# A hybrid decoder trunk: scores between tiles replaced by a recurrent state carried from tile to tile

## The reference

```python
S_t = diag(a_t) S_{t-1} + k_t v_t^T ; o_t = S_t^T q_t
    b = jnp.cumsum(ai, axis=2)
    diff = b[:, :, :, None, :] - b[:, :, None, :, :]
    decay = jnp.exp(jnp.where(causal, diff, -jnp.inf))
    scores = jnp.einsum('bhtc,bhsc,bhtsc->bhts', qi, ki, decay)
    o_intra = jnp.einsum('bhts,bhsv->bhtv', scores, vi)
    o_inter = jnp.einsum('bhtc,bhcv->bhtv', qi * jnp.exp(b), state)
```

## Time and profile before

| | |
|---|---|
| median of 3 runs | 2428.96 us (2427.64 to 2429.24) |
| the profiled execution, its own time | 2428.29 us |
| its span in the profile | 2426.6 us |
| granted TensorE clock, mean | 0.998 |
| TensorE busy | 2393.7 us, 99% |
| VectorE busy | 1939.1 us, 80% |
| ScalarE busy | 1202.9 us, 50% |

### The profile page before, as it was taken

How to read it: one execution, slowest core, us unless ns; L and a number is a source line. 1 busy time by engine, 2 the same in 40 slices (tenths; PEclk the granted TensorE clock), 3 DMA queues, 4 the chain that set the end, 5 groups by cost and what they waited for, 6 DMA issues and landing times.

```text
span 2426.6 us, 34798 instructions
## 1 busy us (share of the span) xinstructions
PE 2393.7 (99%) x13375; PEld 2082.1 (86%) x13375; DVE 1939.1 (80%) x2589; ACT 1202.9 (50%) x1787; POOL 50.7 (2%) x79
## 2 busy tenths in 40 slices
PE   8999999999999999999999999999999999999997
PEld 6888888888777888999999999988888888888885
DVE  6777777788887447988888888899999999995456
ACT  6445444444445235666666666643333333345345
POOL 4000000000000000000000000000000000000111
PEclk9999999999999999999999999999999999999999
DMA  6323323333324234666666666697564575633322
GB/s 176 87 73 82 86 70 85 87 84 81 79 74 152 92 131 137 182 204 200 199 197 196 197 196 196 205 353 253 198 232 160 191 257 195 229 131 116 112 85 99
DMA packets 381406, 373.71 MB, mean 154 GB/s; under 512 B 5532, under 2 KB 311352, under 8 KB 379224
## 3 DMA queue, kind: packets, MB, share of 16 engines
q1 hardware_dynamic: 381240, 371.88, 48.0%
q10 hardware_dynamic: 32, 0.01, 0.0%
HBM read 304.76 MB, written 67.11 MB: 153 GB/s over the span
## 4 chain that ended last, share of the span: by engine, by line
PE 62%; DVE 4%; ACT 1%; issue 1%; DMA 1%; DVEq 0%; ACTq 0%; SPq 0%
PE bank L2323 20%; PE bank L2325 20%; PE bank L2324 20%; DVE w_lo L2064 1%; DMA ring<-in_w_down 0%; DVE h L2110 0%; DVE w_lo L1927 0%; ACT w_hi L1143 0%; DVE w_lo L2201 0%; PE bank L2708 0%; PE bank L2603 0%; DVE gate_e L2227 0%; DVE h L2230 0%; PE bank L2401 0%; ACT gate_inv L1355 0%
## 5 line engine op out<-in xcount | busy, mean ns | idle before, releaser
L2323 PE MATMUL bank<-u_hi,w_hi 128*128 128x512 f32 x896 | 361.8, 404 | 3.4 <-DVE w_lo L1466 2.0
L2323 PE MATMUL bank<-w_hi,forms 128*128 128x512 f32 x896 | 349.4, 390 | 1.1 <-DVE h L2110 1.1
L2325 PE MATMUL bank<-u_hi,w_lo 128*128 128x512 f32 x896 | 349.8, 390 | 0.0
L2324 PE MATMUL bank<-u_lo,w_hi 128*128 128x512 f32 x896 | 349.2, 390 | 0.0
L2325 PE MATMUL bank<-w_hi,forms 128*128 128x512 f32 x896 | 348.7, 389 | 0.0
L2324 PE MATMUL bank<-w_lo,forms 128*128 128x512 f32 x896 | 348.6, 389 | 0.0
L2323 PE MATMUL bank<-xs,w_hi 128*128 128x256 f32 x1024 | 289.9, 283 | 1.4 <-DVE w_lo L1927 0.9
L2324 PE MATMUL bank<-xs,w_hi 128*128 128x256 f32 x1024 | 289.6, 283 | 0.0
L2325 PE MATMUL bank<-xs,w_lo 128*128 128x256 f32 x1024 | 289.5, 283 | 0.0
L1273 ACT ACTIVATE w_hi<-ring 128x1024 fp32r<-128x1024 f32 x124 | 132.0, 1066 | 214.6 <-PE bank L2325 140.4
L1466 DVE TENSOR_TENSOR w_lo<-w_raw,w_hi 128x2048 fp32r<-128x2048 f32 x70 | 160.0, 2286 | 63.2 <-ACT w_hi L874 63.0
(11 more groups left out here) (315 smaller groups left out, 5235.1 us busy)
## 6 DMA issues: line engine op xcount, KB each, us to landing
w_raw<-in_w_in SPq DMA_DIRECT2D x56, 1024.0 KB, 5.6
forms_scratch<-stage SPq DMA_DIRECT2D x32, 1792.0 KB, 11.4
forms<-forms_scratch SPq DMA_DIRECT2D x56, 1024.0 KB, 8.3
ring<-in_w_down SPq DMA_DIRECT2D x39, 1024.0 KB, 5.3
w_raw<-in_w_up SPq DMA_DIRECT2D x32, 1024.0 KB, 7.8
raw<-in_w_up SPq DMA_DIRECT2D x32, 1024.0 KB, 8.0
w_raw<-in_w_down SPq DMA_DIRECT2D x25, 1024.0 KB, 5.1
ring<-in_w_pg SPq DMA_DIRECT2D x18, 1024.0 KB, 5.0
```

What stands on the lines that cost most here:

```text
L2323: pe.matmul(ps, whi, xhi, start=start, stop=False, skip_group_check=shared)
L2324: pe.matmul(ps, whi, xlo, start=False, stop=False, skip_group_check=shared)
L2325: return pe.matmul(ps, wlo, xhi, start=False, stop=stop, skip_group_check=shared)
```

## The change

The scores between tiles are not formed any more. For tiles 0, 1 and 2 the decayed keys are turned by TensorE (`turn_keys`: three transposes and one matmul of a single column, in one group with the late levels and the turned values ahead of tile 4), copied by ScalarE (`place_keys`), and multiplied with the turned values ahead of tile 9 (`sums_of_tiles`, one matmul of 128 or 256 columns for each of the three tiles). VectorE makes of them the state after each tile (`next_states`: a copy and two multiply-adds, behind the clamp of the output gate of `prev`, and in GLA heads behind `alpha_in`). `outputs` multiplies the values by the score matrix of each tile alone and then the states by the decayed queries: seven matmuls of 127 to 129 columns for each 128 value rows. It waits for the states between the two parts.

The queries of all levels are taken one place to the left of where they stood, and the outputs are written one column to the right in `A`: the diagonal becomes part of level 0, and level 0 needs no decay. So the diagonal's four matmuls, its placement, its mask and the reversed copy of keys (`kk_back`) go, as do the difference and exponentials of level 0, whose products become copies. `A` shrinks from 2048 to 520 columns. Renamed semaphores, callers with changed names, and the mask loop of GpSimd without the diagonal are left out here.

```diff
-LATE_AT, CROSS_AT = 4, 7
+LATE_AT, STATE_AT = 4, 9
...
-        kk_back = mx("kk_back", [P, NT // 2, P])
-        kd_back = mx("kd_back", [P, P])
+        kd_back = mx("kd_back", [P, NT // 2, P])
...
-        A = mx("A", [P, NT * S])
+        A = mx("A", [P, S + 8])
+        qd = mx("qd", [P, S])
+        kd_turned = mx("kd_turned", [P, NT - 1, P])
+        states = mx("states", [P, NT - 1, 2 * P])
         V = mx("V", [P, NT, 2 * P])
-        decay01 = mx("decay01", [P, 1])
+        decay = mx("decay", [P, NT - 1, 1])
...
             return t.rearrange("q (n c) -> q n c", c=1 << lv)
-        def diag_blocks(lv=None):
...
+        def queries(t, lv):
+            return t.rearrange("q (n c) -> q n c", c=2 << lv)[:, :, (1 << lv) - 1:(2 << lv) - 1]
+        def level_blocks(lv):
+            return A[:, 0:S].rearrange("q (i n c) -> q i n c", i=NT, c=2 << lv)[:, :, :, 1 << lv:2 << lv]
+        def inner(t):
+            return t[:, P:S].rearrange("q (t c) -> q t c", c=P)[:, :, 0:P - 1]
+        def ends(t, first):
+            return t[:, first * P:(first + NT - 1) * P].rearrange("q (t c) -> q t c", c=P)[:, :, P - 1:P]
+        def sum_of_tile(hd, t):
+            spare = isinstance(hd.h, int) and hd.H == HEADS - 1
...
             def level_exps(hd, levels):
                 for lv in levels:
                     d = tmp[:, lv % 2, :]
-                    act.wait_ge(diff_ready, LEVELS * hd.H + lv + 1)
+                    act.wait_ge(diff_ready, DIFFS * hd.H + lv)
                     act.activation(left(d, lv), left(d, lv), ACT.Exp, scale=-1.0)
                     act.activation(right(d, lv), right(d, lv), ACT.Exp).then_inc(exp_ready, 1)
-            def cross_exps(hd):
...
+            def key_exps(hd):
+                kd = tmp[:, 2, :]
+                for t in range(NT):
+                    last = act.activation(row(kd, t), row(b, t), ACT.Exp, scale=-1.0, bias=b[:, t * P + P - 1:t * P + P])
+                last.then_inc(cross_exp, 1)
+            def query_exps(hd):
+                act.wait_ge(level_ready, LEVELS * (hd.H + 1))
+                act.activation(inner(tmp[:, 0, :]), inner(b[:, :]), ACT.Exp)
+                act.activation(decay[:, :, :], ends(b[:, :], 1), ACT.Exp).then_inc(cross_exp, 1)
+            def place_keys(hd):
+                act.wait_ge(kd_done, hd.H + 1)
                 act.wait_ge(o_done, hd.H)
-                act.activation(A[:, P:2 * P], bank[6][:, 2 * P:3 * P], ACT.Copy)
...
+                act.activation(kd_turned[:, :, :].rearrange("q t c -> q (t c)"), bank[7][:, 0:3 * P], ACT.Copy)
+                act.activation(A[:, S:S + 1], bank[7][:, 3 * P:3 * P + 1], ACT.Copy).then_inc(kd_placed, 1)
...
                 if next_y:
                     next_y()
                 level_exps(hd, range(LEVELS - 1, LEVELS))
-                cross_exps(hd)
+                key_exps(hd)
+                query_exps(hd)
...
-                v.tensor_scalar(back(kk_back[:, :, :]), tiles_of(inverse, 1), minus_one_plus_lb[:, ds(hd.h, 1)], None, ALU.mult)
                 v.tensor_scalar(kk[:], inverse, minus_one_plus_lb[:, ds(hd.h, 1)], None, ALU.mult)\
                     .then_inc(sig_step, 1)
...
-                difference(hd, 0)
                 difference(hd, 1)
+                difference(hd, 2)
...
-                if lv == 0:
+                if lv == 1:
                     v.wait_ge(b_ready, hd.H + 1)
                     v.wait_ge(level_ready, L)
-                    v.wait_ge(cross_done, hd.H)
-                if lv >= 2:
+                    v.wait_ge(qd_ready, hd.H)
+                    v.wait_ge(kd_done, hd.H)
+                if lv >= 3:
                     v.wait_ge(level_ready, L + lv - 1)
                 bv = b[:, :].rearrange("q (n c) -> q n c", c=2 << lv)
                 ref = bv[:, :, (1 << lv) - 1:1 << lv].to_broadcast([P, S // (2 << lv), 2 << lv])
             def level_products(hd, levels):
                 for lv in levels:
+                    if lv == 0:
+                        for odd in range(2):
+                            v.tensor_copy(packed(kl[:, 0, :], 0, odd), left_of_tiles(kk[:, :], 0, odd))
+                        v.tensor_copy(halves(ql[:, 0, :], 0), queries(zq[:, :], 0)).then_inc(level_ready, 1)
+                        continue
                     L = LEVELS * hd.H + lv
                     d = tmp[:, lv % 2, :]
-                    v.wait_ge(exp_ready, L + 1)
+                    v.wait_ge(exp_ready, DIFFS * hd.H + lv)
                     if lv >= 4:
                         v.wait_ge(scores_done, L - 3)
                     for odd in range(2):
                         v.tensor_tensor(packed(kl[:, lv % 4, :], lv, odd), left_of_tiles(kk[:, :], lv, odd),
                                         left_of_tiles(d, lv, odd), ALU.mult)
-                    v.tensor_tensor(halves(ql[:, lv % 4, :], lv), right(zq[:, :], lv), right(d, lv), ALU.mult)\
+                    v.tensor_tensor(halves(ql[:, lv % 4, :], lv), queries(zq[:, :], lv), queries(d, lv), ALU.mult)\
                         .then_inc(level_ready, 1)
                     if lv + 2 < LEVELS:
                         difference(hd, lv + 2)
-            def cross_decay(hd):
...
-                v.wait_ge(level_ready, LEVELS * (hd.H + 1))
...
+            def key_products(hd):
+                v.wait_ge(cross_exp, 2 * hd.H + 1)
+                kd = tmp[:, 2, :]
+                v.tensor_tensor(tiles_of(kd, 0), tiles_of(kd, 0), tiles_of(kk[:, :], 0), ALU.mult)
+                v.tensor_tensor(back(kd_back[:, :, :]), tiles_of(kd, 1), tiles_of(kk[:, :], 1), ALU.mult).then_inc(kd_ready, 1)
+            def query_products(hd):
+                v.tensor_copy(ends(qd[:, :], 0), ends(zq[:, :], 0))
+                v.wait_ge(cross_exp, 2 * hd.H + 2)
+                v.tensor_tensor(inner(qd[:, :]), inner(tmp[:, 0, :]), inner(zq[:, :]), ALU.mult)
+                v.tensor_scalar(qd[:, S - 1:S], zq[:, S - 1:S], decay[:, NT - 2, :], None, ALU.mult).then_inc(qd_ready, 1)
+            def next_states(hd):
+                width = hd.vt * P
+                v.wait_ge(state_done, hd.H + 1)
+                v.tensor_copy(states[:, 0, 0:width], sum_of_tile(hd, 0)).then_inc(state_step, 1)
+                for t in range(1, NT - 1):
+                    v.wait_ge(state_step, 3 * hd.H + t)
+                    v.scalar_tensor_tensor(out=states[:, t, 0:width], in0=states[:, t - 1, 0:width], scalar=decay[:, t - 1, :],
+                                           in1=sum_of_tile(hd, t), op0=ALU.mult, op1=ALU.add).then_inc(state_step, 1)
             def counted(value):
...
                     if lv == 0:
-                        v.wait_ge(diag_placed, cross)
+                        v.wait_ge(o_done, used)
                     v.wait_ge(level_placed, placed)
                     if lv in (0, 2, 3):
                         v.wait_ge(scores_done, scores)
-                    if lv == LEVELS - 1:
-                        v.wait_ge(cross_done, cross)
-                    v.copy_predicated(diag_blocks(lv), masks[:, lv, :].rearrange("q (i n c) -> q i n c", **shape),
+                    v.copy_predicated(level_blocks(lv), masks[:, lv, :].rearrange("q (i n c) -> q i n c", **shape),
                                       bank[bk][:, at:at + 256].rearrange("q (i n c) -> q i n c", **shape))\
                         .then_inc(level_placed, 1)
-            def place_early(hd):
...
                     slot(0)
                     place_levels(prev, range(EARLY, LEVELS))
                     if not hd.gla:
-                        output_gate(prev)
+                        output_gate(prev, {0: lambda: next_states(prev)})
                     elif prev.gla:
-                        output_gate(prev, {0: lambda: alpha_in(hd), 1: lambda: alpha_out(hd)})
+                        output_gate(prev, {0: lambda: (alpha_in(hd), next_states(prev)), 1: lambda: alpha_out(hd)})
                     else:
-                        output_gate(prev, {0: lambda: alpha_in(hd)}, {0: lambda: alpha_out(hd)})
+                        output_gate(prev, {0: lambda: (alpha_in(hd), next_states(prev))}, {0: lambda: alpha_out(hd)})
                 if prev is None:
                     slot(1)
...
                 if next_y:
                     next_y()
                 level_products(hd, range(LEVELS - 1, LEVELS))
-                cross_decay(hd)
                 if hd.gla:
                     evacuate(hd.unit(5), zg[:, 1, :])
-                cross_products(hd)
+                key_products(hd)
+                query_products(hd)
                 if not hd.gla:
                     evacuate(hd.unit(3), zg[:, 0, :])
...
             def out_lo(n):
                 split_lo(Unit(U_OUT + n))
-            output_gate(last, {0: lambda: out_lo(1), 1: lambda: split_y(range(4, 8))})
+            output_gate(last, {0: lambda: (out_lo(1), next_states(last)), 1: lambda: split_y(range(4, 8))})
             out_lo(2)
...
             def early_scores(hd):
```

(71 more changed lines are left out.)

82 lines of the change are left out of this document (14 added, 68 removed).

## The result

The changed kernel takes 2411.97 us (median of 4 runs, 2410.98 to 2413.88), the kernel before 2428.3 beside it (4 runs, 2427.53 to 2429.24). The ratio is 0.9934, with a 95% interval from 0.9916 to 0.9951. It is 16.3 us faster, where 14.8 were forecast; 2411.97 lies in the range of 2408 to 2422. A second measurement follows among the experiments (kernel 5).

The account below looks back on a forecast made before the run. PE was taken to bound HGRN2 heads and DVE's chain GLA heads. Terms 0.89 + 9.4 + 0.2 + 1.0 + 0.6 + 2.1 + 0.64 summed to 14.8 us saved, giving 2414 us; range 2408 to 2422.

Parts of the forecast that it names:

- rival 3: PE's short matmuls cost more, 0.31 us instead of 0.22, adding 13 us: no change, 2426; chance 0.07 with its like.
- The wait for level 1: HGRN2 early group: PE waits about 0.3 us for DVE's level 1 (0 to 0.6), giving back 2.1 us over seven heads.
- The copies of level 0: DVE: copies in place of level 0's products save some 0.15 us over three operations.
- GLA periods: DVE's chain from `alpha_in` to the next unit 0's low part sets them: net -0.3 us each, to 78.7.
- Rival 1: PE alone counts, the GLA chain falling by 1.5 us or more: 19.2 us saved, 2408 to 2410; chance 0.18.
- The 2 us at level 2: GLA heads: PE waits about 2 us at level 2, reaching it 1.5 us sooner and DVE hardly sooner.
- the wait forecast ahead of unit 0: GLA heads: PE was also to wait ahead of unit 0 in the profile after.
- The first period: First GLA period has slack, so PE's own terms count: outputs 0.54 + diagonal 0.89 - gate product 0.44 = 1.0 saved.
- the last head: PE comes 1.3 us earlier and the diagonal's placement (0.83) goes: 2.1 us saved ahead of the first output unit.
- the first quad: -0.44 + 1.08 = 0.64 us saved; the states are made while the sums' tile runs.
- The slower rival: PE waits at tile 9 for late turned keys and values; 3 us late gives 2438; chance 0.06.
- more is given back: Level 1 wait 0.6 us, GLA periods not falling or growing: 10 down to 6 us saved, 2418 to 2423; chance 0.19.

Follow-up runs that it names:

- kernel 5: The changed kernel unaltered, measured once more: 2412.51 us (5 runs) against 2427.66 before; ratio 0.9937.
- experiment 1: Changed kernel with the diagonal's four matmuls put back ahead of level 0, result unused: 2417.64 us.
- experiment 7: kernel 6 with level 1 of HGRN2 heads as its own group ahead of tile 1 of unit 3: 2405.45 us; ratio to before 0.9908.
- experiment 4: Changed kernel with the sums of tiles ahead of tile 5 of unit 0 instead of tile 9: 2420.5 us.
- kernel 2: Changed kernel with each of the three operations that make the states done twice, extra result unused: 2418.22 us.
- kernel 3: Changed kernel with `next_states` ahead of `alpha_in` in all GLA iterations: 2408.23 us.
- kernel 6: kernel 3 with the sums of tiles at tile 8 and the gate product at tile 9: 2407.10 us; ratio to before 0.9915.
- kernel 8: Changed kernel with both the diagonal's matmuls put back and the states' operations done twice: 2421.96 us.

## Why the prediction was right, and where it was not

**HGRN2 heads: right, nearly term by term.** A period of 51.3 was forecast and 51.22 measured, 1.37 less than before. Outputs saved 0.60 (2.08 to 1.48) where 0.54 was said. The diagonal with the early group saved 0.66 (1.77 to 1.11) where 0.89 - 0.3 = 0.59 was said. The two groups in unit 0 saved 0.14 (3.37 to 3.23) where 1.31 - 0.33 - 0.11 - 0.66 = 0.21 was said. The sums look cheaper than 0.66 with their 0.59, but the last step of every group is about 0.08 shorter than the others, and the late levels lost that shorter step when the turns joined them (326.44 - 324.66 = 1.78 where they took 1.71 alone). The short matmuls kept their 0.22, so rival 3 falls. The single-column matmul took 0.14 (326.91 - 326.77), between the stated ends of 0 and 0.22 and near the 0.11 taken. By the Trainium skill (TensorE: Matmul & The Clock Gate, Back-to-back issue gap) it would be an estimated 0.05, two times the floor for small matmuls; the trace has nearly three times that.

**The wait for level 1: right in place and in size, by errors of both signs.** 0.3 was forecast and 0.30 measured (1.11 - 0.81). The copies of level 0 save 0.39 us over three operations and not 0.15: the term rested on the 354 ns of the earlier trace rows, and a plain copy of 256 takes 0.29. Here the rule of the Trainium skill (VectorE: DVE Perf Modes, The perf-mode tier table) was nearer than the row that I preferred to it. So DVE had level 1 ready sooner than forecast: at 309.50 + 0.42 = 309.92, which is 24.86 after the start of the outputs at 285.06, and not 25.1. PE would have come to it at 309.33 + 0.44 = 309.77, 24.7 after the start of the outputs, as forecast. By these two the wait should have been 0.15. The term that was missing is the one between the end of DVE's record and PE at its full pace again; I put it at nothing, and it makes the other 0.15. The kernel before shows the same: by the prediction's own working level 1 was ready 0.08 ahead of PE, and yet the group held 0.07 of waiting, so that "in the HGRN2 heads PE never waits" was a little wrong as well.

The sum gave the wait to seven heads, and only six have it. In head 7 DVE does not wait for its own results in the norm of `prev` (0.24 us in one of its rows in the other heads) and has level 1 ready 24.35 after the outputs began (411.46 + 0.42 - 387.53). Experiments 1 and 7 show that the wait is there: it hid 0.3 of the 0.89 put back, and moving level 1 away took 0.29 off.

**GLA periods: right in size, wrong in the step.** The step that failed is the one that let the chain run "from `alpha_in` to the low part of the next unit 0". It ends at level 2. There PE catches up with DVE, and from there PE alone needs 31.8 us to the next gate product, in both kernels, if the old wait ahead of unit 0 is counted before (31.79; 0.35 of idle time, 0.5 by distances of starts) and the later gate product after (31.77). By the right endpoint the sum has three terms: 1.03 for `next_states` (it takes 1.37, but the distance from `alpha_in` to the silu's next step grew from 1.00 to 2.03 only, as the wait of 0.25 in it went), less 0.46 for `kk_back`, less 1.00 for level 0 (0.61 + 0.39). That is -0.43, against -0.39 measured between gate product and level 2 and -0.42 for the period. My sum counted two terms that lie behind level 2: the diagonal's placement (-0.83), which freed nothing that PE waited for but the end of an old wait, and the later gate product (+0.44). With `next_states` at 1.6 and the copies at 0.15 it came to -0.3: near the truth because errors of both signs met. Rival 1 (PE alone) falls with experiment 1.

The 2 us at level 2 were forecast and came (2.08 and 2.06), but the wait forecast ahead of unit 0 did not: the low part ends just in time.

**The first period and the last head.** -1.0 forecast, -0.94 measured; -2.1 forecast, -2.58 measured; the first quad -0.64 against -0.9. Between the profiled spans 2.3 us more were saved than forecast (17.1 against 14.8): these three make 0.7 of it, the two full periods 0.2, the heads up to the first gate product 0.3 (10.8 against 10.5), which is the wait that head 7 does not have. The rest is the early start of the first unit (0.7), which is not shown to be a gain of the change, and the later stages (0.4), which are none. The medians are 16.3 apart, between runs of the changed kernel that spread over 2.9.

**The slower rival** had its place right and its slack too small: 2.0 us are to spare at tile 9, not 1. The wait begins only when the sums stand some three tiles earlier (2.0 us at 0.68 for a tile), and at tile 5 it costs 9.2 us and leaves 7 of the gain (experiment 4). The rival "more is given back" did not come in this run, but it had a cause that I had not thought of: the clock behind the level 2 wait. It makes the second measurement's profiled run 1.5 us longer in one period.

Not tried: the query shift alone, with cross scores in place of states, so the two halves of the change are separated only by their terms. Open as well: what decides in which place the clock falls behind a wait of 2.1 us.

## What to carry to other kernels

Where two engines lead in turn within a period, find each point where one catches up with the other, and cost a change from one such point to the next: an operation counts only if it lies in the stretch that its own engine leads. Work that one engine saves ahead of such a point becomes a wait there, and the cheapest use of it is to move the other engine's new work out of that stretch. Exchanging two calls and moving two groups by one tile brought 5.4 us here, about a third of what the whole change had brought (in the profiled runs 1.5 of it was time at the lower clock, behind a wait that they took away).

## What the runs showed of the hardware that was not expected

- Behind a wait of 2.1 us at level 2 TensorE's granted clock stood at its lower level for about 3.5 us, in three of the eight such places of the profiled runs (0.52 and 0.62 over stretches of kernel 2, 0.59 over one of the repetition; none in the changed kernel's first run nor in kernel 4). It cost 1.5 us each time (81.2 against 79.7, 80.11 against 78.62), in rows that mark PE as busy. Behind waits of 1.2 us or less at that place it was not seen (kernels 1, 3, 6, 7 and 8).
- A wait inside a group that a row joins shows in no idle time: 0.30 us in each of six heads, to be read only from distances of starts (1.11 against 0.81). The times at which DVE was ready and PE would have come (309.92 and 309.77) account for half of it only.
- A copy of 256 float32 columns took 0.29 us on DVE where the product of two such operands took 0.42 and a one-input operation on a reversed pattern 0.354; as three operations, copies take a little over half the time of products by starts (0.47 and 0.86).
- Where DVE waits for its own last result, the next operation starts later: the rows show 0.15 us of idle time (at 622.55). In the changed kernel the first two operations of a convolution start 0.64 us apart where the row shows this wait (530.62 and 531.26) and 0.52 where it does not (452.77 and 453.29).
